# Routed experts that store rows by token and choice: one transformer layer on one Trainium2 core

## What is computed

```
idx, w = route(h)            # 8 of 64 experts for each token, weights w
y  = (silu(h @ ws1) * (h @ ws3)) @ ws2                                  # shared expert, hidden width 256
y += sum over k of w[k] * (silu(h @ w1[e]) * (h @ w3[e])) @ w2[e]       # e = idx[k]
x  = LN2(ALPHA * x + gate * y)
```

## Time and profile before

| what | us |
|---|---|
| median of 3 runs | 1445.88 |
| lowest and highest run | 1442.6, 1446.25 |
| span of the profiled execution | 1441.5 |
| PE busy in it | 1142.5 (79%) |
| DVE, ACT, POOL busy | 467.1, 249.1, 174.2 |

### The profile page before, as it was taken

How to read it: one execution, slowest core, us unless ns; L and a number is a source line. 1 busy time by engine, 2 the same in 40 slices (tenths; PEclk the granted TensorE clock), 3 DMA queues, 4 the chain that set the end, 5 groups by cost and what they waited for, 6 DMA issues and landing times. The chain is left out here.

```text
span 1441.5 us, 23491 instructions
## 1 busy us (share of the span) xinstructions
PE 1142.5 (79%) x7919; PEld 741.4 (51%) x7920; DVE 467.1 (32%) x873; ACT 249.1 (17%) x502; POOL 174.2 (12%) x284
## 2 busy tenths in 40 slices
PE   3299999996685799586888887999867698778763
PEld 2197787784564344343555544555544454444421
DVE  4324323337843114774222221222211121111246
ACT  1122212325454000101111111111111011011000
POOL 0001211100000000002120111101110110110055
PEclk9999999996789799787999999999999899898987
DMA  8575786438363861193469899998799999999774
GB/s 290 122 269 193 252 272 216 156 132 295 111 201 108 299 189 69 57 415 103 153 199 376 332 345 387 376 391 294 267 368 372 371 381 379 384 382 380 321 257 151
DMA packets 120488, 382.58 MB, mean 265 GB/s; under 512 B 14501, under 2 KB 31845, under 8 KB 95726
## 3 DMA queue, kind: packets, MB, share of 16 engines
q1 hardware_dynamic: 105742, 338.12, 64.9%
q0 software_dynamic: 12960, 40.53, 9.1%
q10 hardware_dynamic: 1728, 3.15, 0.6%
HBM read 335.37 MB, written 46.37 MB: 265 GB/s over the span
## 5 line engine op out<-in xcount | busy, mean ns | idle before, releaser
L1561 PE MATMUL PS<-W,XT 128*64 128x256 f32 x2048 | 263.0, 413 | 85.5 <-DMA W<-w 83.0
L1561 PEld LDWEIGHTS PS<-W,XT 128*64 128x64 f32 x2048 | 179.6, 149 | 191.9 <-issue 137.9
L1610 PE MATMUL PS<-W,hidT 128*64 128x512 f32 x512 | 124.0, 605 | 2.8 <-DVE hidT L1679 2.0
L1679 DVE COPY hidT<-PS 128x128 f32<-128x128 f32 x64 | 18.7, 292 | 311.6 <-PE PS L1602 310.8
L425 DVE TENSOR_TENSOR w_lo<-raw,w_hi 128x2048 fp32r<-128x2048 f32 x26 | 59.5, 2289 | 148.4 <-ACT w_hi L387 148.4
L1632 ACT ACTIVATE sg<-PS 64x256 f32<-64x256 f32 x64 | 24.2, 378 | 445.3 <-PE PS L1561 445.3
L358 PE MATMUL PS<-w_hi,u_hi 128*128 128x512 f32 x240 | 95.6, 398 | 0.0
L358 PE MATMUL PS<-w_hi,u_lo 128*128 128x512 f32 x240 | 94.8, 395 | 0.0
L358 PE MATMUL PS<-w_lo,u_hi 128*128 128x512 f32 x240 | 94.7, 395 | 0.0
L1575 PE MATMUL PS<-W,XTo 128*64 128x256 f32 x736 | 84.5, 381 | 7.3 <-DVE Yo L1673 6.7
L1575 PEld LDWEIGHTS PS<-W,XTo 128*64 128x64 f32 x736 | 60.4, 137 | 39.8 <-issue 25.5
(11 more groups left out here) (314 smaller groups left out, 1470.6 us busy)
## 6 DMA issues: line engine op xcount, KB each, us to landing
W<-w SPq DMA_DIRECT2D x192, 1024.0 KB, 12.5
raw<-w_in SPq DMA_DIRECT2D x26, 1024.0 KB, 9.1
expert_rows<-Y SPq DMA_DIRECT2D x128, 128.0 KB, 9.1
oaT<-w_ada SPq DMA_DIRECT2D x8, 1536.0 KB, 7.7
expert_rows<-zeros SPq DMA_DIRECT2D x23, 512.0 KB, 6.7
expert_rows<-Yo SPq DMA_DIRECT2D x46, 128.0 KB, 2.9
obT<-w_ada SPq DMA_DIRECT2D x8, 512.0 KB, 8.1
kc<-cache_k_diff SPq DMA_DIRECT2D x8, 512.0 KB, 4.6
```

The source lines that it names most:

```text
L1561: mm = pe.matmul(PS[64 * h:64 * h + 64, 2 + i % 2, 0:F], XT[:, i % 2, k], t.W13[:, i, h, k], start=k == 0, stop=k == KD - 1)
L1610: mm = pe.matmul(PS[64 * h:64 * h + 64, 5 + i % 2], hidT[:, i % 2, j], t.W2[:, i, j, CW * h:CW * h + CW], start=j == 0, stop=j == 1)
```

## The change

- Padded slots get a number far out of bounds, and gathers and stores with a bound check leave them out. The first four experts and the first extra block still gather row 0 for padded slots.
- `y_dram` holds 3072 x 2 half rows of 512 numbers at the place of (token, choice, half). POOL stores Y and Yo with one indirect DMA of 128 half rows each (a scatter), whose row numbers `t.dest` come from the list matmuls; these are now float32, run twice (for PSUM rows 0 to 63 and 64 to 127), and list `1 + 8 * token + choice`. `t.rows` goes.
- POOL's order in the body of n: scatter of n-1, gather for n+4, then for each extra block the next extra gather and the scatter of the extra block before it. Ahead of the loop it scatters nothing once, after it the last extra block.
- SP stores nothing. It loads w1 and w3 of n+4 (`load_up`) once h_mm shows expert n's w1/w3 matmuls done and o_h those of its extra blocks, and w2 of n+4 (`load_down`, two DMAs) after the w2 matmuls of n and its last extra eviction.
- w1 and w3 go side by side into 128 columns for each half of PSUM's rows, so that SiLU, product and transpose of the middle layer work on 128 x 128 instead of 64 x 256; w2 is loaded in rows of 4 KB. The extra blocks share these PSUM tiles, and wait for the previous Yo only ahead of their w2 matmuls.
- The `vec` loads move from routing to the start of SP's part of experts, since `CB` lies in vec's memory.
- Combine loads 12 plain DMAs of 1 MB (two choices of a tile each) from SP into buffers for all three tiles.
- The zero fill goes.

```diff
@@ attention_prompt, SP
-            sp.wait_ge(t.zeros_done, 1)
-            fills = range(E * SLOTS, NBLK * SLOTS, P)
...
-            sp.wait_ge(rows_zero, 16 * len(fills))
@@ loads
+def load_up(sp, t, e, i):
...
+def load_down(sp, t, e, i):
+
+    for k in range(2):
+        src = t.w2v[e, :, k] if isinstance(e, int) else t.w2v[bass.ds(e, 1), :, k].rearrange("e p n -> (e p) n")
+        sp.dma_start(t.W2[:, i, k], src).then_inc(t.wdn_in[i], 16)
@@ routing, PE and DVE
                 for k in range(TOPK):
-                    mm = pe.matmul(PS[0:SLOTS, 5, 0:NBLK], SL[:, n % 2, k], CB[:, n % 2, k], start=n + k == 0, stop=n == NT - 1 and k == TOPK - 1)
+                    for h in range(2):
+                        mm = pe.matmul(PS[SLOTS * h:SLOTS * h + SLOTS, 5, 0:NBLK], SL[:, n % 2, k], CB[:, n % 2, k],
+                                       start=n + k == 0, stop=n == NT - 1 and k == TOPK - 1)
...
-                link(dve.tensor_tensor(CBf[:, :, :], io[:, 0:NBLK].unsqueeze(1).to_broadcast([P, TOPK, NBLK]),
-                                       cf[:, :].unsqueeze(2).to_broadcast([P, TOPK, NBLK]), ALU.is_equal))
-                dve.tensor_scalar(CB[:, n % 2], CBf[:, :, :], tk[:, n:n + 1], None, ALU.mult).then_inc(code_done, 1)
+                for k in range(TOPK):
+                    ins = dve.tensor_scalar(CB[:, n % 2, k], io[:, 0:NBLK], cf[:, k:k + 1], val[:, n, k:k + 1], ALU.is_equal, ALU.mult)
+                ins.then_inc(code_done, 1)
+
             dve.wait_ge(list_mm, NT)
+            listed = PS[:, 5, 0:NBLK]
+            link(dve.tensor_scalar(far[:, :], listed, 0.0, FAR, ALU.is_equal, ALU.mult))
+            link(dve.scalar_tensor_tensor(dest_f[0:SLOTS, :], listed[0:SLOTS], -1.0, far[0:SLOTS, :], ALU.add, ALU.add))
+            for c0, c1 in ((0, WB), (E, E + 1)):
+                link(dve.tensor_scalar(dest_f[0:SLOTS, c0:c1], listed[0:SLOTS, c0:c1], -1.0, 0.0, ALU.add, ALU.max))
+            link(dve.tensor_copy(t.tokens[:, 0:NBLK], dest_f[0:SLOTS, :]))
             link(dve.memset(t.tokens[:, NBLK:NBLK + 1], 0))
-            dve.tensor_copy(t.tokens[:, 0:NBLK], PS[0:SLOTS, 5, 0:NBLK])
+            link(dve.tensor_scalar(t.tokens[:, :], t.tokens[:, :], 3, None, ALU.logical_shift_right))
+            link(dve.scalar_tensor_tensor(dest_f[:, :], listed, 2.0, far[:, :], ALU.mult, ALU.add))
+            link(dve.memset(t.dest[:, E:E + 1], 1 << 20))
+            link(dve.tensor_scalar(t.dest[:, 0:E], dest_f[:, 0:E], half[:, 0:1], None, ALU.add))
+            dve.tensor_scalar(t.dest[:, E + 1:NBLK + 1], dest_f[:, E:NBLK], half[:, 0:1], None, ALU.add)
@@ experts, SP
             def body(it, i, last):
...
+                n = at(it, i)
                 if not last:
-                    load_expert(sp, t, at(it, i, WB), i)
...
+                    done = sp.value_load(t.ov[0:1, bass.ds(n + 1, 1)], min_val=0, max_val=XB)
+                    sp.wait_ge(h_mm, n + 1)
+                    stand_alone(sp)
+                    sp.wait_ge(o_h, done + 1)
+                    stand_alone(sp)
+                    load_up(sp, t, at(it, i, WB), i)
+                    sp.wait_ge(yy_mm, n + 1)
+                    stand_alone(sp)
+                    sp.wait_ge(o_ye, done + 1)
+                    stand_alone(sp)
+                    load_down(sp, t, at(it, i, WB), i)
@@ experts, POOL
+            def scatter(n, i, before):
+                once_above(pool, y_out[i % 2], before * 16)
+                pool.tensor_copy(dx[:, i % 2:i % 2 + 1], t.dest[:, bass.ds(n, 1)]).then_inc(dx_done, 1)
+                pool.wait_ge(dx_done, n + 1)
+                pool.wait_ge(yy_ev, n + 1)
+                stand_alone(pool)
+                pool.indirect_dma_start(t.y_dram, bass.IndirectOffsetOnAxis(ap=dx[:, i % 2:i % 2 + 1], axis=0), Y[:, i % 2], None,
+                                        bounds_check=TOK * TOPK * 2 - 1, oob_is_err=False).then_inc(y_out[i % 2], 16)
...
             def body(it, i, last):
-                extra(pool, at(it, i), gather_next)
+                if not isinstance(it, int) or it > 0 or i > 0:
+                    scatter(at(it, i, -1), i - 1, it * (WB // 2) + (i - 1) // 2)
                 if not last:
                     pool.wait_ge(xt_mm, at(it, i, 1))
                     gather(at(it, i, WB), i, at(it, i, WB + 1))
+                extra(pool, at(it, i), step)
@@ experts, PE
-                        mm = pe.matmul(PS[64 * h:64 * h + 64, 2 + i % 2, 0:F], XT[:, i % 2, k], t.W13[:, i, h, k], start=k == 0, stop=k == KD - 1)
+                        mm = pe.matmul(PS[64 * h:64 * h + 64, 2 + i % 2, 0:F].rearrange("s (w f) -> s w f", w=2), XT[:, i % 2, k],
+                                       t.W13[:, i, :, k, P * h:P * h + P], start=k == 0, stop=k == KD - 1)
...
                     pe.wait_ge(o_xe, g + 1)
-                    pe.wait_ge(o_ye, g + 1)
@@ combine, SP
+            rows = t.y_dram.rearrange("(n p k h) c -> n p k (h c)", p=P, k=TOPK, h=2)
+            for n in range(NT):
+                for j in range(PAIRS):
+                    sp.dma_start(G[:, n, 2 * j:2 * j + 2], rows[n, :, 2 * j:2 * j + 2]).then_inc(pair_in[n][j], 16)
```

## The result

The changed kernel takes 1424.18 us (median of 4 runs, 1419.84 to 1430.16) against 1444.24 (4 runs, 1438.37 to 1446.25): ratio 0.9867, 95% interval 0.9824 to 0.991. The forecast was 1412, the range 1380 to 1434. The profiled execution took 1428.14 us, with a span of 1426.3. I compare spans: 1426.3 - 1441.5 = -15.2, where the sum said -34. The medians are 20.1 us apart.

A forecast was written before the change was run, and what follows sets the result against it. PE was taken to bound the experts up to 1047 us, DMA from there to 1345. Start +8.8, PE's half -8, DMA's half -33, last store +1.5, combine -3 sum to -34: 1412 us, range 1380 to 1434.

The forecast's parts named there:

- DMA's half: Experts stage from 1047 us on, where DMA is the bound: -33 us, from earlier loads and shorter steps.
- Two thirds of 0.89: Each expert step in the DMA-bound part: skipping 36 of 64 slots saves at most 0.89 us; 0.6 taken.
- The rival of the crowding low slots: Gather's busiest DMA engines keep their load, the scatter's half: 0.35 us saved a step, -25 us, 1420; chance 0.22.
- The head start: Entering the DMA-bound part: earlier weight loads let up(32) start at about 1048.3 instead of 1062.4 us.
- PE's half: Experts stage up to 1047 us, PE-bound: -31 from waits removed, against late extra gathers; net -8 us (-31 to +10).
- The rival in which everything lands early: Extra gathers land in 4 us, full 0.89 saved a step, no contention at the end: -72, 1374; chance 0.18.
- The first gather beside vec: Start of the experts: the first gather reaches PE 0 to 3.7 us later beside 2 MB of vec; 1.5 taken.
- DVE's chain: Behind routing's last list: 11 linked DVE instructions instead of 2, +2.3 us, all on the path.
- the +5 for the lists: Routing's float32 list matmuls, 3.0 us each, of which roughly two show: +5 us (2 to 8).
- The last scatters: End of the experts stage: two scatters replace the last store, one copy, gap and issue more: +1.5 us.
- Combine: Last part of the kernel: 62 us against 65, -3, with PE's products still slowed beside POOL's.
- POOL as a bound: Rival in the experts stage: scatter issue of 6 us makes POOL need 774 us, kernel 1518; chance 0.06.

The follow-up runs named there:

- the two repeats: The changed kernel run again unaltered, in two later sets beside the kernel before: 1425.19 us (ratio 0.9849) and 1427.63 us (0.9864).
- full gather: Against the changed kernel, padded slots fetch row 0 again while the scatter still skips them: 1468.26 us, ratio 1.0209 to the kernel before.
- spread slots: Filled slots spread over all 64 instead of the lowest: on the changed kernel 1420.47 us; on the one with late vectors, early extra gather, swapped last scatters 1389.82 us.
- the old load order: Against the changed kernel, all weights of expert n+4 load only after expert n's eviction, as before the change: 1455.40 us, ratio 1.0112.
- the late vectors: Against the changed kernel, the vec loads move from the start of SP's experts part to behind its last weight load: 1416.15 us, ratio 0.9795.

## Why the prediction was right, and where it wasn't

The bound, the order of the parts and the sign held, and the time lies within the range. Step by step:

- **DMA's half: right, by sizes that made up for each other, which was luck.** The step fell by 0.58 (from 9.57 to 8.99) and by 0.64 in the two repeats; I took 0.6. The experiments show of what it is made. Skipping gathered rows saves 9.60 - 8.93 = 0.67 a step in the changed kernel, more than the 0.5 of their bytes. Skipping scattered rows saves 0.28, less than the 0.69 * 36/64 = 0.39 of theirs. The two together make 0.95, if they add, and 0.6 was won. Of the 0.3 between them there are two explanations: the scatter is dearer than the plain store that it replaces, or a full gather costs more in the changed kernel than it did before, where it ran at 381 GB/s. No run separates them. "Two thirds of 0.89" was thus a good number with a wrong reason: neither a skipped slot's turn nor crowding took the other third.
- **The rival of the crowding low slots is wrong.** Two kernels with spread slots show no gain in time (8.82 and 8.93 a step, ratios 0.9875 and 0.9646 against 0.9864 and 0.9643). The Trainium skill, page "DMA: Bandwidth & Descriptors", section "The descriptor swizzle", gives each engine two groups of four neighbouring partitions in a transfer of 128; the runs neither bear out nor exclude that order for these gathers and scatters, they only show that spreading the slots wins no time.
- **The head start: its size was right, its place and its cause not.** Mark 30 to 34 fell by 14.1 us, as forecast. But the forecast had up(32) start at 1048.3, 4.7 us behind up(30), and called PE no bound there; PE's own steps forbid that. up(32) now comes 12.6 us behind up(30), 18.8 before: 6.2 won there, and the rest by the experts behind it. As for the cause, with the old load order this part is 29.9 us, 4 more than the changed kernel's 26.0, and with the full gather 32.8, 7 more. So both have a part in it, the skipped gathers the larger one, and 3 to 4 of the 14 us come back in neither run. The load order gives 20 to 25 us in PE's half, and few of them as waits for weights (4.4).
- **PE's half: the waits held, one term was missing.** Between the up-matmuls of experts 1 and 30 the waits for weights, for the product and for Yo fell by 29.2 us (12.8, 9.7 and 6.7; forecast 31), and 16.9 us for XGo came (forecast 23, with the second blocks). The missing term is slow matmuls: PE is busy 8.7 us longer, 6.7 of it in the w2 matmuls of extra blocks. -29.2 + 16.9 + 8.7 = -3.6, measured -4.3. I had counted "the slowed matmuls behind them" where waits go, and not where they come. In the whole stage the same matmuls are busy 53.0 us, and 44.6 where the waits are gone.
- **The rival in which everything lands early** didn't come: the extra gathers were late by 20.4 us in the whole stage, and the contention in combine was there (three products took 8.02 and 8.00 us, forecast 8.1).
- **The first gather beside vec: the step that failed most.** I took 1.5 us out of 0 to 3.7, with the landing on a loaded queue as the upper end. It cost 8, and the late vectors give it back; beside it the vec loads moved at 4.1 us a MB. The upper end came from the nearest row, but that row was of another kind of load. Of the two other terms of the start, DVE's chain held (from 671.23 to 673.78). So did the +5 for the lists, which end 4.6 us later than before, but by luck: not two lists of 3.0 us show but all three, of 3.23, 1.75 and 1.75.
- **The last scatters: mis-sized.** +1.5 was a copy, a gap and an issue. The gap from the last eviction to combine grew from 4.4 to 11.6 us, +7.2. I priced the second scatter's issue but took the way from an indirect transfer to the next block to be as short as from the plain store. The 5.9 us behind an empty one say otherwise.
- **Combine: right**, 61.4 against 62. Tile 0's sum starts 17.8 us in (forecast 18).
- **POOL as a bound: wrong.** The scatter's issue takes 1.01 us, and POOL is busy 81 of 285 us.

By the starts of the up-matmuls the misses are +7.5 for the start (the gather +6.6, the terms ahead of it -0.6, the rest in the second gather's 2.06 us and slow first matmuls), +3.7 for PE's half, +0.3 for DMA's and +7.0 for the end (the gap +5.7, and 1.7 for expert 63's up-matmuls, which took 5.36 us instead of 3.67). Together 18.5, from -33.7 to -15.2.

One of the signs that I had named failed with this: up(30) is not level with before but 12 us later, since the start gave away more than PE's half won.

The fastest kernel of the runs, 0.9643 of the kernel before, keeps everything of the change. It moves the vectors behind the loop and the extra gather to the head of POOL's queue.

## What to carry to other kernels

A transfer that is late at a point where PE has no other work can cost more than its wait, because of the slow matmuls behind it. So what the bounding engine needs soonest goes to the head of the issuing queue, ahead of anything that waits for an eviction. Look what else is issued in the microsecond before the first gather of a stage: a load that nobody needs for 600 us can hold up rows that are needed at once. When skipping bytes, price the gathered and the scattered side apart, and price the last transfer of a stage by the time from its issue to the next block, not by its issue alone.

## What the runs showed of the hardware

- In the changed kernel gathered rows cost more than bytes: adding some 36 of 64 padded 4 KB rows back took 0.67 us a step and lowered the DMA's total from 381 to 386 GB/s down to 366, whichever row they read. Adding the same bytes to the scatter left 387 GB/s and took 0.28 us. The kernel before gathered all its rows at 381 GB/s beside plain stores.
- A skipped row still leaves a packet: the changed kernel and the one with the full gather have 108761 packets each, but 18698 instead of 16181 of them are under 512 B, and 349.77 instead of 360.07 MB move. That is 2517 small packets for 10.3 MB, about one for each row of 4 KB.
- An indirect store whose 128 rows are all out of range was followed by the next block only 5.9 us after the end of its issue, against 8.1 us with its rows.
- The broadcast loads of vec took 4.1 us a MB beside the gathers (weights 2.6), and vec stretched the landing of gathers beside them from 3.8 to 12.9 us.
- After 4.26 us without work PE ran eight matmuls in 3.68 us at a granted clock of 0.50 that take 1.94 at 1.00, and was back at 1.94 some 10 us later.
